# Values and output gates of a gated linear attention block as plain fp32 products by token rows, in place of three fp32r products of split weights

## Chip, cores and metric

One core of one Trainium2 chip. The metric is the device time of one execution in microseconds; the median of three runs of the kernel before is 1797.29 us (1794.79 to 1800.07).

## What is computed

A two-layer hybrid block, then a second two-layer block, on 256 tokens of width 1024, all in fp32. The change lies in one mixer of the second block, the gated linear attention (GLA), 4 heads with key width 128 and value width 256:

```python
def gla_mixer(h, w_in, w_alpha, b_alpha, norm_g, w_out):
    proj = h @ w_in
    q, k, v, r, z = jnp.split(proj, [GLA_QK, 2 * GLA_QK, 2 * GLA_QK + D_MODEL, 2 * GLA_QK + 2 * D_MODEL], axis=-1)
    log_alpha = jax.nn.log_sigmoid((z @ w_alpha + b_alpha).astype(jnp.float32)) / GLA_TAU
    ...
    o = gla_chunk_scan(q, k, v, log_alpha)
    o = rmsnorm_2(o, norm_g).reshape(bsz, s, D_MODEL).astype(h.dtype)
    return (o * jax.nn.silu(r)) @ w_out
```

`v` and `r` (the output gate) are each `h` (256 x 1024) times a 1024 x 1024 part of `w_in`.

## The kernel before

Activations lie in SBUF feature-major: `[128 partitions, feature tile k of 8, tokens]`. Dense products run as **three fp32r products**: an operand is split into a high half (fp32r, written by a cast) and a low half (the rest), and high x high, high x low and low x high are summed in PSUM.

**Weights.** SyncE streams 1 MB slabs of 256 output columns (`stream`, DMA at line 1273) into a ring of `RING = 3` slots, in the order of use; slab n waits until slab n - 3 is marked used (line 1272). A slab is two units of 128 columns. `split_to` on ScalarE copies a unit to `w_hi` (line 1314), `split_to` on VectorE writes `w_lo` (line 2025) and marks the slab used at its second half. There are `PARTS = 4` slots for halves: unit u waits until TensorE has used unit u - 4. `split_until(tile)` runs the split up to `AHEAD = 3` units ahead of a tile; an explicit `split_to(unit_of[...])` fixes the place in an engine's queue by hand. Every engine's queue is one list in program order; all waits are on counters of finished steps.

**TensorE's side.** `project(name, n)` (line 639, products at 653, 655, 658) waits for the unit's halves and makes a 128 x 256 result, feature-major, in 24 products. `open_bank` (line 586) takes the eight PSUM banks in turn and waits until the name eight before has been emptied. `keep_clock(n)` (line 598, products at 604) issues n plain fp32 products whose result nobody reads. `turn_tokens` (line 686, transposes at 691) transposes a 128-column tile into token rows.

**The GLA block, in TensorE's order.** `project_group` of glaq 0 to 2 with z (lines 1107 to 1123); the four `alpha` products (1128); glaq 3 and glak 0 to 3; then glav 0 to 7, each `project`, evacuated to `act_t`, turned by `turn_tokens` and evacuated to `gv`; then eight level products `lev` (lines 1139 to 1158, 1152 the main one) with a cross product per head (1162) and after every second one a gate chunk glar 0 to 3; then the head products `go` (1182, 1183), feature-major, with the sums of squares through a product by ones (`head_squares`, 1170); then glar 4 to 7; `keep_clock(7)`; and `block_out("gla")`, which is `rows_out` with `by_tile=True`: `two_chunks` (1008 to 1010) runs output chunks 0 and 1 tile by tile as the input tiles get ready, then the loop at 1039 to 1041 chunks 2 and 3. Then the boundary to the feed-forward, `gain_rows` and `ffn(1)`.

**ScalarE's side** (lines 1888 to 1943): z, then weight halves up to glak 1, Abs of the four alphas, Exp, Ln, and only then the evacuation of glaq 0 to 3 and of the keys; for the values an evacuation, the evacuation of the turned tile and one level factor's Exp (1913) each; Silu of the gates; copy and square of the heads (1930, 1931); the roots; Silu of gates 4 to 7; the high halves of the eight output tiles (1769).

**VectorE's side** (lines 2868 to 2959): log forget gates and their scans (2883, 2886), level differences (2902, 2903) and level factors (2911, 2912) with weight halves at fixed places between, masks and sums of the level products (2924 to 2934), four reciprocals of 128 x 256 (2940), the norm with gain (2944), the product with the gate (2953), the low halves (2033), and the storing of output rows.

Of the kernel before, what the change touches and what calls it, by code (L numbers as in the profile page):

```python
# [25 lines left out]
P = 128  # L26
# [86 lines left out]
def program(nc, io, counts):  # L113

    ctx = ExitStack()
    with ctx:
# [157 lines left out]
        yT, sq8 = carve(0, KT, S), carve(2048, KT, S)  # L274
# [10 lines left out]
        zT, scan_one = carve(17408, S), carve(17664, S)  # L285
        ff_act = carve(4096, FT, S)
# [242 lines left out]
        for n, c0, k in (("q", 0, 2), ("k", 512, 2), ("v", 1024, 4), ("r", 2048, 4)):  # L529
            for i in range(k):  # L530
                split_cols(f"w gla{n} {i}", [f"gla{n} {2 * i + j}" for j in range(2)], io["gla_w_in_2"][0],
                           c0 + 256 * i, "gla")
# [44 lines left out]
        def _(pe):  # L577
# [447 lines left out]
            def rows_out(tag, chunks, part, ready, by_tile):  # L1025
# [43 lines left out]
            def block_out(tag):  # L1069

                rows_out(tag, block_chunks(tag), lambda h, k: h[:, k, S:2 * S], both_parts(tag), True)
# [61 lines left out]
            for n in range(KT):  # L1133
                project(f"glav {n}", S)
                if n:
                    turn_tokens(f"glav {n - 1}", act_t[(n - 1) % 2], ST)
            turn_tokens(f"glav {KT - 1}", act_t[(KT - 1) % 2], ST)

            for n in range(GLA_H * ST):
# [24 lines left out]
                if n % 2 == 0:  # L1164
                    project(f"glar {n // 2}", S)
            def head_squares(hd):
                out = open_bank(f"gs {hd}")
                for e in range(2):
                    pe.wait_ge(*scalar.did(f"go {2 * hd + e}"))
                    m = pe.matmul(out[:, 0:S], ones_pp, sq8[:, 2 * hd + e, :], start=e == 0, stop=e == 1)  # L1170
                m.then_inc(*tensor.does(f"filled gs {hd}"))

            pe.wait_ge(*scalar.did("gv 7"))
            for hd in range(GLA_H):
# [3 lines left out]
                for e in range(2):  # L1178
                    name = f"go {2 * hd + e}"
                    out = open_bank(name)  # L1180
                    c = 256 * hd + P * e
                    pe.matmul(out[:, 0:S], gv[:, 0, c:c + P], attT[:, hd, 0, :], start=True, stop=False)
                    pe.matmul(out[:, P:S], gv[:, 1, c:c + P], attT[:, hd, 1, P:S], start=False, stop=True)\
                        .then_inc(*tensor.does("filled " + name))
                if hd:
                    head_squares(hd - 1)
            head_squares(GLA_H - 1)

            for n in range(KT // 2, KT):
                project(f"glar {n}", S)  # L1190
            keep_clock(7)
            block_out("gla")
# [99 lines left out]
        def _(act):  # L1292
# [614 lines left out]
            for i in range(8):  # L1907
                projected(f"glav {i}", act_t[i % 2][:, 0:S], also=[f"rows glav {i}"])
                if i:
                    evacuate(f"turned glav {i - 1}", gv[:, :, P * i - P:P * i], also=[f"gv {i - 1}"])  # L1910
                j = (7 + i) % 8
# [3 lines left out]
            evacuate(f"turned glav {KT - 1}", gv[:, :, D - P:D], also=[f"gv {KT - 1}"])  # L1915
            def r_out(n):
                projected(f"glar {n}", r_sil[:, n, :], ACT.Silu, [f"r_sil {n}"])
# [7 lines left out]
            warm_sqrt("gs")  # L1925
            for n in range(KT):
                name = f"go {n}"
                act.wait_ge(*tensor.did("filled " + name))

                nc.scalar.activation(gla_o[:, n, :], bank(name)[:, 0:S], ACT.Copy)  # L1930
                nc.scalar.activation(sq8[:, n, :], bank(name)[:, 0:S], ACT.Square)\
                    .then_inc(*scalar.does(name, "emptied " + name))
            for hd in range(GLA_H):
                evacuate(f"gs {hd}", act_t[hd][:, 0:S], ACT.Sqrt, [f"dev gs {hd}"], scale=1.0 / (2 * P), bias=eps)
            for n in range(KT // 2, KT):
                r_out(n)
            split_to(unit_of["y gla.3"])
            for n in range(KT):
                high_tile("gla", gla_o, "gla_y", n)
# [7 lines left out]
        def _(dve):  # L1947
# [931 lines left out]
            split_to(unit_of["glak 1"])  # L2879
# [4 lines left out]
            for hd in range(GLA_H):  # L2884
                after(f"lb {hd}")
                step(nc.vector.tensor_tensor_scan(gg[:, hd, :], scan_one, la[:, hd, :], 0.0, ALU.mult, ALU.add), f"gg {hd}")
            after(f"gg {GLA_H - 1}")
# [8 lines left out]
            for n, i in enumerate(level_order):  # L2896
                split_to(unit_of["glaq 0"] + 5 + n)
# [8 lines left out]
            for n, i in enumerate(level_order):  # L2906
                split_to(min(unit_of["glaq 0"] + 11 + n, unit_of["glar 1"]))
# [8 lines left out]
            for n in range(GLA_H * ST):  # L2916
                hd, t = n // ST, n % ST
                if n % 2 == 0:
                    split_for(f"glar {n // 2}")
# [16 lines left out]
            split_for(f"glar {KT // 2 - 1}")  # L2936
            settled()
            for hd in range(GLA_H):
                dve.wait_ge(*scalar.did(f"dev gs {hd}"))
                step(nc.vector.reciprocal(dve_t[hd][:, 0:S], act_t[hd][:, 0:S]), f"rinv gs {hd}")  # L2940
            split_for(f"glar {KT // 2}")
            for n in range(KT):
                after(f"rinv gs {n // 2}")
                step(nc.vector.scalar_tensor_tensor(gla_o[:, n, :], gla_o[:, n, :], param("gla_g")[:, n % 2:n % 2 + 1],
                                                    dve_t[n // 2][:, 0:S], ALU.mult, ALU.mult), f"gon {n}")
                if n == 3:
                    split_for(f"glar {KT // 2 + 1}")
            for n in range(KT):
                if KT // 2 + 1 < n:
                    split_for(f"glar {n}")  # L2950
                dve.wait_ge(*scalar.did(f"r_sil {n}"))
                after(f"gon {n}")
# [105 lines left out]
```

## Time and profile before

| | us |
|---|---|
| median of three runs (lowest, highest) | 1797.29 (1794.79, 1800.07) |
| the profiled execution, its own time | 1796.44 |
| span of that execution, first to last instruction | 1794.7 |
| TensorE busy (share of the span) | 1731.7 (96%) |
| VectorE busy | 1428.3 (80%) |
| ScalarE busy | 884.1 (49%) |
| weight streams, share of 16 engines' span | 50.7% |

The profile is of one execution. A matmul record's duration holds its latency; what a product costs in a run of them is the distance of the starts. A plain fp32 product shows as two records, an fp32r product as one. The clock column is the granted clock of TensorE as a share of 2.4 GHz.

### The profile page before, as it was taken

Reading aid. Unit: us, or ns where it says so; the run is one execution under the profiler, and the core shown is the slowest. Engines: PE = TensorE matmul, PEld = TensorE weight load, DVE = VectorE, ACT = ScalarE, POOL = GpSimd, SP = SyncE. Lnnn points to the kernel's source line nnn. Section 1 sums busy time; section 2 is a strip of 40 time slices with the busy share of each in tenths; the row PEclk is TensorE's granted clock in tenths of the full one; section 3 lists DMA queues with packets and bytes.
Section 4 is the critical chain, followed back from the end, with each engine's and each line's share of the span. In section 5 each row is a group of like instructions: output and inputs, shape, how many; then the busy total and the mean of one; then the engine's idle time right before and its main releaser. Section 6 shows DMA issues by size and latency. Waiting matters only on the chain.

```text
span 1794.7 us, 29926 instructions
## 1 busy us (share of the span) xinstructions
PE 1731.7 (96%) x11446; PEld 1536.0 (86%) x11446; DVE 1428.3 (80%) x2579; ACT 884.1 (49%) x1560; POOL 0.2 (0%) x4
## 2 busy tenths in 40 slices
PE   6999999999999999999999999998999989999998
PEld 3788887767888887888978999988999989899998
DVE  7799996558899898887876899877988468768874
ACT  4322334456223233453356745676666466556653
POOL 0000000000000000000000000000000000000000
PEclk9999999999999999999999999999999999999999
DMA  9583321211767776643522499544555535236553
GB/s 341 194 289 109 94 71 32 87 37 63 265 231 252 256 253 214 206 149 117 165 71 84 143 339 311 193 147 142 164 190 174 179 118 165 94 103 204 188 171 112
DMA packets 242189, 301.44 MB, mean 168 GB/s; under 512 B 6000, under 2 KB 223472, under 8 KB 241664
## 3 DMA queue, kind: packets, MB, share of 16 engines
q1 hardware_dynamic: 242048, 299.52, 50.7%
q8 instruction: 93, 1.52, 0.4%
q14 instruction: 48, 0.39, 0.1%
HBM read 298.45 MB, written 1.05 MB: 167 GB/s over the span
## 4 chain that ended last, share of the span: by engine, by line
PE 44%; DVE 7%; ACT 3%; issue 2%; DMA 0%; DVEq 0%; ACTq 0%
PE bank L653 10%; PE bank L655 10%; PE bank L658 10%; PE bank L1039 2%; PE bank L1040 2%; PE bank L1041 2%; DVE w_lo L2025 2%; ACT w_hi L1314 1%; PE bank L629 1%; PE bank L630 1%; PE bank L631 1%; DVE xT L2659 0%; PE bank L874 0%; PE bank L1093 0%; PE bank L897 0%
## 5 line engine op out<-in xcount | busy, mean ns | idle before, releaser
L2025 DVE TENSOR_TENSOR w_lo<-ring,w_hi 128x1024 fp32r<-128x1024 f32 (+2 forms) x444 | 499.4, 1133 | 184.5 <-ACT w_hi L1314 183.4
L1314 ACT ACTIVATE w_hi<-ring 128x1024 fp32r<-128x1024 f32 (+2 forms) x444 | 432.5, 984 | 179.6 <-PE bank L658 97.7
L653 PE MATMUL bank<-h_hi,w_hi 128*128 128x256 f32 (+2 forms) x2270 | 406.3, 321 | 3.9 <-ACT arena L1300 3.6
L655 PE MATMUL bank<-h_lo,w_hi 128*128 128x256 f32 (+2 forms) x2270 | 397.7, 317 | 0.0
L658 PE MATMUL bank<-h_hi,w_lo 128*128 128x256 f32 (+2 forms) x2270 | 396.8, 316 | 0.1
L653 PEld LDWEIGHTS bank<-h_hi,w_hi 128*128 128x128 f32 x2270 | 333.7, 189 | 39.6 <-ACT arena L1300 4.8
L655 PEld LDWEIGHTS bank<-h_lo,w_hi 128*128 128x128 f32 x2270 | 334.5, 189 | 29.8
L658 PEld LDWEIGHTS bank<-h_hi,w_lo 128*128 128x128 f32 x2270 | 333.3, 188 | 30.2 <-DVE w_lo L2025 0.5
L1300 ACT ACTIVATE work<-bank 128x512 f32<-128x512 f32 (+1 forms) x142 | 70.3, 512 | 257.5 <-PE bank L658 204.6
L1300 ACT ACTIVATE arena<-bank 128x256 f32<-128x256 f32 (+4 forms) x125 | 56.4, 454 | 206.9 <-PE bank L658 147.5
L2332 DVE SCALAR_TENSOR_TENSOR arena<-arena,params 128x512 f32<-128x512 f32 (+1 forms) x240 | 130.3, 610 | 0.0
L2062 DVE CUSTOM_DVE_ANT_0 arena<-arena,c_row,params 128x1024 f32<-128x1024 f32 x96 | 119.8, 1279 | 3.2 <-DMA arena<-in_ada_w_t 3.2
L1039 PE MATMUL bank<-w_hi,h_hi 128*128 128x256 f32 x320 | 90.0, 281 | 2.9 <-ACT w_hi L1314 2.6
L1300 ACT ACTIVATE work<-bank,params 128x256 f32<-128x256 f32 x88 | 49.5, 563 | 85.6 <-DVE w_lo L2025 43.1
L1041 PE MATMUL bank<-w_hi,h_lo 128*128 128x256 f32 x320 | 90.0, 281 | 0.0
L1040 PE MATMUL bank<-w_lo,h_hi 128*128 128x256 f32 x320 | 89.9, 281 | 0.0
L653 PE MATMUL bank<-arena_r,w_hi 128*128 128x512 f32 (+2 forms) x306 | 64.8, 338 | 1.9 <-ACT w_hi L1314 1.7
L2735 DVE SCALAR_TENSOR_TENSOR work<-bank,params,work 128x255 f32<-128x255 f32 x88 | 42.3, 481 | 29.2 <-ACT work L1300 29.2
L655 PE MATMUL bank<-arena_r,w_hi 128*128 128x512 f32 (+2 forms) x306 | 64.6, 337 | 0.0
L658 PE MATMUL bank<-arena_r,w_lo 128*128 128x512 f32 (+2 forms) x306 | 64.5, 337 | 0.0
L1039 PEld LDWEIGHTS bank<-w_hi,h_hi 128*128 128x128 f32 x320 | 60.2, 188 | 3.7 <-ACT w_hi L1314 3.0
L2058 DVE CUSTOM_DVE_ANT_0 arena<-arena,tables,params 128x1024 f32<-128x1024 f32 x48 | 60.5, 1279 | 0.0
(312 smaller groups left out, 2292.0 us busy)
## 6 DMA issues: line engine op xcount, KB each, us to landing
ring<-in_w_in SPq DMA_DIRECT2D x86, 1024.0 KB, 5.8
arena<-in_ada_w_t SPq DMA_DIRECT2D x96, 512.0 KB, 6.0
ring<-in_ffn_w_up SPq DMA_DIRECT2D x44, 1024.0 KB, 5.1
ring<-in_w_branch SPq DMA_DIRECT2D x32, 512.0 KB, 4.9
arena<-in_w_mod_t SPq DMA_DIRECT2D x32, 512.0 KB, 5.5
ring<-in_ffn_w_down SPq DMA_DIRECT2D x16, 1024.0 KB, 5.1
ring<-in_gla_w_in SPq DMA_DIRECT2D x12, 1024.0 KB, 5.3
ring<-in_w_out SPq DMA_DIRECT2D x8, 1024.0 KB, 6.4
```

The source lines that it names most:

```text
L653: pe.matmul(out[:, 0:n], w[0][:, k, :], hi(k, n), start=k == 0, stop=False)
L655: pe.matmul(out[:, 0:n], w[0][:, k, :], lo(k, n), start=False, stop=False)
L658: m = pe.matmul(out[:, 0:n], w[1][:, k, :], hi(k, n), start=False, stop=k == tiles - 1)
L1039: pe.matmul(out, part(h_hi, k)[:, rows], hi, start=k == 0, stop=False)
L1040: pe.matmul(out, part(h_hi, k)[:, rows], lo, start=False, stop=False)
L1041: return pe.matmul(out, part(h_lo, k)[:, rows], hi, start=False, stop=k == k1 - 1 and k1 == chunks(c)[-1][1])
L1300: return nc.scalar.activation(dst, src, func, **kw)\
L1314: nc.scalar.activation(w_hi[u % PARTS][:, 0:src.shape[1], :], src, ACT.Copy)\
L2025: step(nc.vector.tensor_tensor(w_lo[u % PARTS][:, 0:nk, :], src, w_hi[u % PARTS][:, 0:nk, :].bitcast(F32), ALU.subtract), f"lo {u}", *(["u ...
L2058: step(nc.vector.tensor_tensor_reduce(w if v else scratch, w, c_rows[:, v, :], 1.0, param("b_mod", 2)[:, l, c:c + 1], ALU.mult, ALU.add, m ...
L2062: step(nc.vector.tensor_tensor_reduce(w, w, c2_row, 1.0, param("ada_b", 2)[:, l, c:c + 1], ALU.mult, ALU.add, mod2[l][:, c:c + 1]), name)
L2332: step(nc.vector.scalar_tensor_tensor(dst, src, cw[:, l, k, n:n + 1], dst, ALU.mult, ALU.add), name)
```

## The change

- The slabs of values and gates are no longer split: they are put in the stream as they are, without units, and TensorE marks them used.
- `project_rows(kind, i)`: token rows t of chunk c (256 columns) as 8 plain fp32 products, the normed activations `pair_tile(k)` stationary and the slab moving; the result is already by token rows, 128 x 256. All values (8) and all gates (8) go so; the transposes of the values go.
- Heads are computed by token rows, 3 products of 256 columns each. Their sums of squares come from ScalarE's accumulator over a row, so root and reciprocal are on 128 x 8. The gate and the norm are one VectorE step from PSUM (for head 3 two steps).
- The heads are turned back by transposes (`head_turned`), between gates 5, 6, 7, and for head 3 inside the first output chunk; high and low halves are made from PSUM with the norm gain. `keep_clock(7)` goes. `block_out` uses the plain chunk loop for all four chunks (`by_tile` false).
- ScalarE empties glaq 0 to 2 ahead of the alphas; the weight halves of the keys stand at other places; ScalarE's and VectorE's splits for values and gates go.

```diff
-        gla_o = carve(4096, KT, S)
+        gla_o = carve(4096, ST, D)
-        r_sil = carve(11264, KT, S)
+        r_sil = carve(11264, ST, D)
...
+                if n in "vr":
+                    stream.append((f"w gla{n} {i}", by_rows(io["gla_w_in_2"][0])[:, :, c0 + 256 * i:c0 + 256 * i + 256], (8, 256)))
+                else:
+                    split_cols(f"w gla{n} {i}", [f"gla{n} {2 * i + j}" for j in range(2)], io["gla_w_in_2"][0],
+                               c0 + 256 * i, "gla")
...
+                        early = k1 - 2 if between and c == 0 else k0
+                        for t in range(ST if early > k0 else 0):
+                            for k in range(k0, early):
+                                if t == 0:
+                                    ready(k)
+                                products(k, t)
+                            if t == 0:
+                                between()
                         for t in range(ST):
-                            for k in range(k0, k1):
+                            for k in range(early, k1):
...
-            for n in range(KT):
-                project(f"glav {n}", S)
-                if n:
-                    turn_tokens(f"glav {n - 1}", act_t[(n - 1) % 2], ST)
-            turn_tokens(f"glav {KT - 1}", act_t[(KT - 1) % 2], ST)
+            def project_rows(kind, i):
+                c, t = i // ST, i % ST
+                w = take(f"w {kind} {c}")
+                out = open_bank(f"{kind} {i}")
+                for k in range(KT):
+                    m = pe.matmul(out[:, 0:2 * P], pair_tile(k)[:, P * t:P * t + P], w[:, k, :],
+                                  start=k == 0, stop=k == KT - 1)
+                m.then_inc(*tensor.does(f"filled {kind} {i}", *([f"used w {kind} {c}"] if t == ST - 1 else [])))
+            for i in range(GLA_H * ST):
+                project_rows("glav", i)
...
-                    project(f"glar {n // 2}", S)
+                    project_rows("glar", n // 2)
+            def head_turned(hd):
+                pe.wait_ge(*vector.did(f"gla_y {hd}.{ST - 1}"))
+                for n in range(2 * hd, 2 * hd + 2):
+                    out = open_bank(f"gla turned {n}")
+                    for t in range(ST):
+                        m = pe.transpose(out[:, P * t:P * t + P], gla_o[:, t, P * n:P * n + P], ident)
+                    m.then_inc(*tensor.does(f"filled gla turned {n}"))
...
+                pe.matmul(out[:, 0:256], attT[:, hd, 0, 0:P], gv[:, 0, v], start=True, stop=True)
+                pe.matmul(out[:, 256:512], attT[:, hd, 0, P:S], gv[:, 0, v], start=True, stop=False)
+                pe.matmul(out[:, 256:512], attT[:, hd, 1, P:S], gv[:, 1, v], start=False, stop=True)\
+                    .then_inc(*tensor.does(f"filled go {hd}"))
+            project_rows("glar", 4)
+            project_rows("glar", 5)
+            head_turned(0)
+            head_turned(1)
+            project_rows("glar", 6)
+            head_turned(2)
+            project_rows("glar", 7)
+            block_out("gla", lambda: head_turned(GLA_H - 1))
```

ScalarE:

```diff
-            split_to(unit_of["glak 1"])
+            split_to(unit_of["glak 0"])
+            for n in range(GROUP):
+                q_out(n)
             for hd in range(GLA_H):
                 evacuate(f"alpha {hd}", le[:, hd, :], ACT.Abs, [f"le {hd}"], last=False,
                          bias=param("gla_b")[:, hd:hd + 1])
+            split_to(unit_of["glak 1"])
...
+            split_to(unit_of["glak 2"])
...
+            split_to(unit_of["glak 3"])
+            q_out(GROUP)
             for n in range(GLA_H):
-                projected(f"glaq {n}", gq[:, n, :], also=[f"gq {n}"], scale=GLA_DK ** -0.5)
-            for n in range(GLA_H):
-                projected(f"glak {n}", gk[:, n, :], also=[f"gk {n}"])
+                evacuate(f"glak {n}", gk[:, n, :], also=[f"gk {n}"])
+            level_exp(0)
+            level_exp(1)
+            for i in range(8):
+                evacuate(f"glav {i}", gv[:, i % 2, rows_of(i)], also=[f"gv {i}"])
+                if i < 3:
+                    level_exp(2 * i + 2)
+                    level_exp(2 * i + 3)
...
+                    nc.scalar.activation(act_t[t][:, 0:S], bank(f"go {hd}")[:, 256 * t:256 * t + 256], ACT.Square,
+                                         accum_out=head_sums[:, i:i + 1]).then_inc(*scalar.does(f"head sum {i}"))
+            act.wait_ge(*scalar.did("head sum 7"))
+            nc.scalar.activation(head_dev, head_sums, ACT.Sqrt, scale=1.0 / (2 * P), bias=eps).then_inc(*scalar.does("head dev"))
+            r_out(4)
+            r_out(5)
+            for n in range(4):
+                turned_high(n)
             split_to(unit_of["y gla.3"])
+            r_out(6)
+            turned_high(4)
+            turned_high(5)
+            r_out(7)
+            turned_high(6)
+            turned_high(7)
```

VectorE (the `split_to` and `split_for` calls between differences, factors, level products, norm and gate are taken out):

```diff
+            dve.wait_ge(*scalar.did("head dev"))
+            step(nc.vector.reciprocal(head_inv, head_dev), "head inv")
...
+            for hd in range(2):
+                for t in range(ST):
+                    head_scaled(hd, t)
+            for t in range(ST):
+                last_head(t)
+            for t in range(ST):
+                head_scaled(2, t)
+            for n in range(4):
+                turned_low(n)
             split_to(unit_of["y gla.3"])
+            last_gated(0)
+            turned_low(4)
+            turned_low(5)
+            last_gated(1)
+            turned_low(6)
+            turned_low(7)
```

`head_scaled` takes a head's bank times the reciprocal times the Silu of the gate into `gla_o`; `turned_high` and `turned_low` make the halves of a turned bank times the norm gain; `last_head` and `last_gated` do head 3 in two steps.

## Rows read from the trace of the kernel before

**Rows 1.** The page: the span, and busy time of each engine.

```profile
span 1794.7 us, 29926 instructions
...
PE 1731.7 (96%) x11446; PEld 1536.0 (86%) x11446; DVE 1428.3 (80%) x2579; ACT 884.1 (49%) x1560; POOL 0.2 (0%) x4
```

**Rows 2.** Busy time of each engine by stretch of the GLA block.

```profile
core 0: us, PE busy (x) PEld busy (x) DVE busy (x) ACT busy (x) POOL busy (x), PEclk, DMA share, GB/s
...
1468.50:1488.10 19.60, 16.04 (x121) 15.86 (x121) 16.70 (x26) 13.16 (x24) 0.00 (x0) 0.91 0.35 108
1488.10:1515.60 27.50, 24.83 (x212) 24.39 (x210) 23.18 (x32) 23.38 (x37) 0.00 (x0) 1.00 0.62 192
1515.60:1539.30 23.70, 23.70 (x344) 22.21 (x345) 19.34 (x41) 8.34 (x18) 0.00 (x0) 0.93 0.27 90
1539.30:1548.00 8.70, 8.70 (x50) 7.71 (x49) 1.97 (x6) 7.25 (x22) 0.00 (x0) 1.00 0.01 2
1548.00:1559.50 11.50, 11.50 (x99) 11.47 (x98) 11.50 (x14) 7.11 (x11) 0.00 (x0) 1.00 0.25 80
1559.50:1566.30 6.80, 3.18 (x17) 2.50 (x15) 6.80 (x14) 5.12 (x11) 0.00 (x0) 1.00 0.39 127
1566.30:1591.00 24.70, 24.55 (x193) 24.37 (x194) 12.58 (x24) 9.33 (x23) 0.00 (x0) 0.93 0.46 151
```

**Rows 3.** Who TensorE waited for from 1440 to 1640 us: total, times, longest.

```profile
PE bank L1008 <- DVE h_lo L2033: 3.6, 1, 3.6
PE bank L653 <- ACT arena L1300: 3.6, 1, 3.6
PE bank L1152 <- ACT w_hi L1314: 2.4, 1, 2.4
```

**Rows 4.** Engine busy time in three shorter stretches, columns as rows 2.

```profile
1475.17:1478.66 3.49, 3.49 (x17) 3.49 (x18) 3.46 (x7) 2.56 (x5) 0.00 (x0) 0.51 0.06 16
1567.40:1570.70 3.30, 3.30 (x18) 3.30 (x17) 1.13 (x4) 0.00 (x0) 0.00 (x0) 0.50 0.90 305
1171.70:1191.00 19.30, 15.12 (x71) 12.45 (x70) 13.21 (x25) 14.66 (x31) 0.00 (x0) 1.00 0.12 37
```

**Rows 5.** TensorE in order of time: start, duration, line, tiles, records.

```profile
1479.61 1.11 PE L653 MATMUL bank<-h_hi,w_hi 128*128 128x256 f32 x8
...
1488.13 1.11 PE L653 MATMUL bank<-h_hi,w_hi 128*128 128x256 f32 x8
...
1493.81 0.38 PE L691 MATMUL bank<-tables,work 128*128 128x128 f32 x2
1493.95 1.19 PE L653 MATMUL bank<-h_hi,w_hi 128*128 128x256 f32 x8
...
1521.16 0.92 PE L1152 MATMUL bank<-arena 128*64 128x64 f32 x24
...
1523.73 1.21 PE L653 MATMUL bank<-h_hi,w_hi 128*128 128x256 f32 x8
...
1526.75 0.92 PE L1152 MATMUL bank<-arena 128*64 128x64 f32 x24
...
1559.48 3.19 PE L604 MATMUL bank<-tables 128*128 128x256 f32 x14
```

**Rows 6.** Groups of instructions, 1455 to 1600 us: busy us, mean ns.

```profile
L2025 DVE TENSOR_TENSOR w_lo<-ring,w_hi 128x1024 fp32r<-128x1024 f32 x33 | 39.9, 1218 | 16.9 <-ACT w_hi L1314 16.8
L1314 ACT ACTIVATE w_hi<-ring 128x1024 fp32r<-128x1024 f32 x32 | 33.3, 1053 | 13.5 <-PE bank L1010 10.1 <-PE bank L1041 3.4
...
L2902 DVE TENSOR_TENSOR arena<-arena 128x512 f32<-128x512 f32 x8 | 5.5, 685 | 0.0
...
L2940 DVE RECIPROCAL work<-work 128x256 f32<-128x256 f32 x4 | 6.6, 1710 | 6.7 <-ACT work L1300 6.7
```

**Rows 7.** Weight slabs (line 1273), 1400 to 1600 us, from issue.

```profile
DMA to landing us min/median/max: 4.3/5.2/6.8
```

**Rows 8.** ScalarE in order of time.

```profile
1471.76 1.28 ACT L1900 ACT_TABLE_LOAD   x1
```

More of the change, by code:

```diff
@@ L1023, in two_chunks, with rows_out @@
                         products(1, k, t)
-            def rows_out(tag, chunks, part, ready, by_tile):
+            def rows_out(tag, chunks, part, ready, by_tile, between=None):
                 if by_tile:
@@ L1177, in _ @@
                 pe.wait_ge(*scalar.did(f"cross {hd}"))
[L1178 to L1192, printed above, removed]
+                out = open_bank(f"go {hd}")
+                v = slice(256 * hd, 256 * hd + 256)
+                pe.matmul(out[:, 0:256], attT[:, hd, 0, 0:P], gv[:, 0, v], start=True, stop=True)
[10 more added lines that the diff above has]
+            block_out("gla", lambda: head_turned(GLA_H - 1))
             gain_rows("ffn 1")
@@ L1924, in _ @@
                     r_out(n // 2)
[L1925 to L1932, printed above, removed]
-            for hd in range(GLA_H):
-                evacuate(f"gs {hd}", act_t[hd][:, 0:S], ACT.Sqrt, [f"dev gs {hd}"], scale=1.0 / (2 * P), bias=eps)
-            for n in range(KT // 2, KT):
-                r_out(n)
-            split_to(unit_of["y gla.3"])
-            for n in range(KT):
-                high_tile("gla", gla_o, "gla_y", n)
+            for hd in range(GLA_H):
+                for t in range(ST):
+                    i = ST * hd + t
+                    act.wait_ge(*tensor.did(f"filled go {hd}"))
+                    if i:
+                        act.wait_ge(*scalar.did(f"head sum {i - 1}"))
+                    nc.scalar.activation(act_t[t][:, 0:S], bank(f"go {hd}")[:, 256 * t:256 * t + 256], ACT.Square,
[6 more added lines that the diff above has]
+                turned_high(n)
+            split_to(unit_of["y gla.3"])
+            r_out(6)
[4 more added lines that the diff above has]
+            turned_high(7)
             warm_sqrt("gla")
@@ L2948, in _ @@
[L2948 to L2952, printed above, removed]
-                step(nc.vector.tensor_tensor(gla_o[:, n, :], gla_o[:, n, :], r_sil[:, n, :], ALU.mult), f"gla_y {n}")
-            split_to(unit_of["y gla.3"])
-            for n in range(KT):
-                low_part(f"gla.{n}", h_lo[:, n, S:2 * S], gla_o[:, n, :], h_hi[:, n, S:2 * S])
+            dve.wait_ge(*scalar.did("head dev"))
@@ new lines, in _, with head_scaled @@
+            step(nc.vector.reciprocal(head_inv, head_dev), "head inv")
+            after("head inv")
+            def head_scaled(hd, t):
+                i = ST * hd + t
+                v = slice(256 * hd, 256 * hd + 256)
+                dve.wait_ge(*scalar.did(f"r_sil {i}"))
+                step(nc.vector.scalar_tensor_tensor(gla_o[:, t, v], bank(f"go {hd}")[:, 256 * t:256 * t + 256],
+                                                    head_inv[:, i:i + 1], r_sil[:, t, v], ALU.mult, ALU.mult),
+                     f"gla_y {hd}.{t}", *([f"emptied go {hd}"] if t == ST - 1 else []))
@@ new lines, in turned_low, with last_head @@
+            def turned_low(n):
+                dve.wait_ge(*scalar.did(f"hi gla.{n}"))
+                step(nc.vector.scalar_tensor_tensor(h_lo[:, n, S:2 * S], bank(f"gla turned {n}")[:, 0:S],
+                                                    param("gla_g")[:, n % 2:n % 2 + 1], h_hi[:, n, S:2 * S].bitcast(F32),
+                                                    ALU.mult, ALU.subtract), f"lo gla.{n}", f"emptied gla turned {n}")
+            def last_head(t):
+                i, v = ST * 3 + t, slice(768, 1024)
+                step(nc.vector.tensor_scalar(gla_o[:, t, v], bank("go 3")[:, 256 * t:256 * t + 256], head_inv[:, i:i + 1],
+                                             None, ALU.mult), f"last head {t}", *(["emptied go 3"] if t == ST - 1 else []))
@@ new lines, in last_gated @@
+            def last_gated(t):
+                v = slice(768, 1024)
+                dve.wait_ge(*scalar.did(f"r_sil {ST * 3 + t}"))
+                after(f"last head {t}")
+                step(nc.vector.tensor_tensor(gla_o[:, t, v], gla_o[:, t, v], r_sil[:, t, v], ALU.mult), f"gla_y 3.{t}")
+            for hd in range(2):
[3 more added lines that the diff above has]
+                last_head(t)
+            for t in range(ST):
+                head_scaled(2, t)
```

53 lines of the change are left out of this document (18 added, 35 removed).

## The prediction

> **What bounds the kernel now.** I read the page first: TensorE is busy 96% of the span [rows 1], so a microsecond is worth something only if it leaves TensorE's queue or an idle gap in it. Then the stretches of the gated linear attention (GLA) block [rows 2]. Read there the gap between a stretch's length and its PE column, and the granted clock: three stretches lose idle time (3.6, 2.7 and 3.6 us), and three show a clock of 0.91 to 0.93. Then who ended the idle gaps [rows 3]: 3.6 us for a bank that ScalarE empties late, 2.4 us ahead of the level products, 3.6 us for the low halves ahead of the output projection. Each gap is followed by a stretch of work at a granted clock of 0.51 and 0.50, 1.2 GHz instead of 2.4 [rows 4] (two of the three are shown; the third falls into the levels). Last the order of time on TensorE [rows 5], for the price of each kind of product. ScalarE and VectorE are not the bound as sums, but they hand over late at these three places.
>
> **Two prices.** A `project` (24 fp32r products, 256 columns, a 128x256 result) repeats every (1488.13 - 1479.61)/3 = 2.84 us, or 0.118 us a product [rows 5]. A plain fp32 product of 256 columns is two records; fourteen records of `keep_clock` take 3.19 us, so one record is (3.19 - 0.38)/13 = 0.216 us and a product 0.432 us [rows 5]. `project_rows` does 8 of them for a result of the same size: 3.46 us. So each of the 16 value and gate chunks becomes 0.62 us **dearer** on TensorE, 9.9 us in all. The recurrent block runs such products with the ring as an operand at clock 1.00 [rows 4], so I take full speed.
> The Trainium skill (FP8 and Floating Point Precision, TensorE Precision Notes) says that true fp32 takes four passes through the array, where the change gives up three. That speaks against the change; the two records of 0.216 us agree in kind, at 0.432 us against 3 x 0.118 = 0.354 us.
>
> **Part by part**, on the path through TensorE.
> 1. Queries and keys, 19.6 us from 1468.5 to 1488.1 [rows 2]. ScalarE now empties glaq 0 to 2 ahead of Abs, Exp and Ln, so glak 0 finds its bank free, and the 3.6 us gap and the slow stretch behind it go. Does the next weight half come late instead? By ScalarE's order: glak 1's high half ends near 1470.1, then a table load of 1.28 us [rows 8], Exp, glak 2's half near 1473.8, load, Ln, glak 3's half near 1477.6. TensorE, running through, wants them at 1474.2, 1477.1 and 1479.9. VectorE's low half of glak 3 waits for the scans, near 1480.6; the third pass wants it at 1481.8. All hold, the last by 1.2 us. Five tiles x 2.84 = 14.2: **-5.4 us**.
> 2. Values, 27.5 us from 1488.1 to 1515.6 [rows 2]: 8 x 3.46 = 27.7 us, without eight pairs of transposes (0.14 us each [rows 5]) and the 2.7 us of gaps. **+0.2 us**. The level factors must be ready at 1510.4: VectorE starts the differences near 1480.6, and 32 half-tile steps at a pitch near 0.6 us (0.685 us long each [rows 6]) end near 1500. Ten microseconds to spare, since its weight halves of 1.22 us [rows 6] have left.
> 3. Levels with gates 0 to 3, 23.7 us [rows 2]: gates +4 x 0.62 = 2.5 us; the slow start goes. The first level and gate take 5.6 us there (1515.6 to 1521.2), against 3.0 for a gate (1523.7 to 1526.8) and 1.1 for a level at full clock [rows 5]: -1.5 us. **+1.0 us**.
> 4. Head products, 8.7 us [rows 2]: four heads x three products x 0.432 = 5.2 us. The eight products of the sums of squares (3.5 us) go to ScalarE. **-3.5 us**.
> 5. Gates 4 to 7, 11.5 us [rows 2]: 13.8 us, 12 transposes x 0.07 = 0.8 us between them, and one wait: gate 6 takes go 2's bank, which VectorE frees only after gate 5's Silu, some 0.7 us late. **+3.9 us**.
> 6. Clock keeping and the wait for the low halves, 6.8 us [rows 2, 3]: both go. The chain behind the heads loses four reciprocals of 1.71 us [rows 6] for one on eight columns, and is now cut into heads: 0 to 2 are ready under gates 6 and 7. **-6.8 us**.
> 7. Output projection, 24.7 us [rows 2]: 192 products x 0.118 = 22.65 us, the last head's four transposes 0.3 us, some 0.4 us for tiles 4 and 5 and the last head, 0.4 us as now at chunk changes; about 1.5 us of it was the slow stretch at 1567 to 1571 [rows 4]. **-0.9 us**.
> The 16 halves taken from ScalarE (1.05 us) and VectorE (1.22 us) [rows 6] count nothing themselves: TensorE's products hide them; they are the slack on which 1, 2 and 6 live. **Slabs**: the value and gate slabs are now held until TensorE has used them, 6.9 us each. A ring of three leaves two slabs' work, about 13.8 us, for a transfer of 4.3 to 6.8 us [rows 7], so no starvation. SyncE's queue has one critical place: output slab 1 is issued when gate 5 is done (1547.3) and lands near 1552.5. Behind it ScalarE waits with halves 2 and 3, and queued behind those is gate 6's Silu, then tiles 4 and 5: ready near 1557.5, when TensorE, which starts at 1555.8, has four tiles of the chunk done.
> Sum: -5.4 + 0.2 + 1.0 - 3.5 + 3.9 - 6.8 - 0.9 = **-11.5 us**. The feed-forward behind it shifts as it stands. The profiled execution took 1796.4 us around a span of 1794.7, 0.9 us under the median of 1797.3. So 1784.9 for that execution, 1785.8 as a median.
> Bounds of what no row shows: the gap in part 5 is between 0 and 1.5 us; the handovers in 7 between 0 and 5 us; the plain pitch with the ring's 1 KB rows as the moving operand between 0.432 and 0.472 us (next part).
>
> **Rivals.**
> A. **The last heads hand over late** (0.12). Against: the estimate above with a median landing. For: four engines pass the last two heads around, and each wait of today's block ended on just such a handover [rows 3]. A landing of 6.8 us instead of 5.2 [rows 7] costs 1.6 us at tiles 4 and 5; the same again for a second exposed hop of head 3, and if the gaps bring half clock, 1.5 us as today, make 4.7 with a table load of 1.28 [rows 8] 6.0 us: 1791.8.
> B. **Plain products cost four times the fp32r pitch** (0.05): 4 x 0.118 = 0.472 us, 16 x 8 x 0.040 = 5.1 us more: 1790.9. Against: the measured 0.216 a record [rows 5]. The rule of four passes in the Trainium skill (FP8 and Floating Point Precision) would give this if each pass had the fp32r overhead; the row shows that it has not.
> C. **Slower: the granted clock falls in the plain stretches** (0.05). Place: values and gates, 16 x 3.46 = 55 us of plain products. Each microsecond of full-clock work costs one more at 1.2 GHz, so it eats the gain from 11.5 us of it, and over 0.3% is reached at 17. If the eight values run so: +27.7, 1813. For: every gap in this block was followed by half clock [rows 4]. Against: products of this kind ran at 1.00 through gaps of 2 us [rows 4], and the new stretch has none.
> D. **The front gains nothing** (0.08): a half of glak 1 to 3 is late by what the bank was. The 1.2 us margin of part 1 is the thin one; if the Ln chain is 3 us later, 1.8 us and the half clock of 1.6 us come back, and part of the 2.4 us gap ahead of the levels: some 5 us, 1790.8.
> That the change does not do what it says I leave out: the order of each queue is written out.
>
> **Numbers.** Forecast 0.70, A 0.12, D 0.08, B 0.05, C 0.05. A measurement of this kernel can tell about 0.3%, 5.4 us, from no change: faster means under 1791.9. The forecast case, with handovers of up to 5 us and spread of the runs (1794.8 to 1800.1) around it, lies there with 0.67 of its 0.70; D and B with 0.09 of 0.13; A with half of 0.12: 0.82. Same 0.13, slower 0.05. Range: 1781.5 (no gap anywhere, 2 us of spread, and the slow stretches and changes of chunk all gone) to 1792.5 (A and the better part of D and B).
>
> **What would show it.** Right: records of the new products 0.216 us apart at clock 1.00; no wait of TensorE over 1 us between 1455 and the output projection's end, which falls near 1579.5 instead of 1591; level products from 1510, heads from 1535, the output projection from 1556; weight halves 16 fewer on both engines. Wrong: a wait on w_hi or w_lo in the keys (D), on gla_o, h_lo or w_hi around tiles 4 to 7 (A), a pitch near 0.236 (B), a clock under 0.9 in the values (C).

## The result and the profile after

The changed kernel takes **1785.39 us** in the median (1782.98 to 1786.30, four runs) against 1797.32 (1794.79 to 1800.07) for the kernel before: a ratio of 0.9931, 95% interval 0.9913 to 0.9949. That is 11.9 us less, where 11.5 were forecast. The profiled execution has a span of 1784.3 us against 1794.7. Its GLA block begins 1.5 us later than in the execution before. That start also varies between kernels that differ in nothing ahead of the block: the first alpha product stands at 1466.13 to 1469.09 in three variants of the changed kernel (exponentials spread, last head turned early, clock keeping put back, all below). So the block is best read by its own length: from the first product of glaq 3 to the first of the gain rows it is 122.5 us before (1468.51 to 1590.97) and 110.6 after (1469.98 to 1580.61), -11.8 us. What follows the block takes 203.7 us in both. The two block lengths come from one profiled execution each.

The page of the changed kernel, the lines that answer to [rows 1], and the two groups of weight halves:

```profile
span 1784.3 us, 29504 instructions
...
PE 1732.5 (97%) x11280; PEld 1530.7 (86%) x11280; DVE 1402.2 (79%) x2554; ACT 865.0 (48%) x1532; POOL 0.2 (0%) x4
...
L2075 DVE TENSOR_TENSOR w_lo<-ring,w_hi 128x1024 fp32r<-128x1024 f32 (+2 forms) x428 | 479.7, 1129 | 183.2 <-ACT w_hi L1336 181.9
L1336 ACT ACTIVATE w_hi<-ring 128x1024 fp32r<-128x1024 f32 (+2 forms) x428 | 415.5, 981 | 177.1 <-PE bank L662 98.7
```

TensorE is busy for 1732.5 us, not for less than before; its share rose because the span fell. The two engines that make the halves have 16 fewer each (444 before).

Busy time by stretch, as [rows 2] (columns as there):

```profile
core 0: us, PE busy (x) PEld busy (x) DVE busy (x) ACT busy (x) POOL busy (x), PEclk, DMA share, GB/s
1469.98:1484.20 14.22, 14.22 (x122) 14.22 (x121) 10.76 (x18) 10.23 (x19) 0.00 (x0) 1.00 0.30 86
1484.20:1511.92 27.72, 27.72 (x131) 24.13 (x129) 17.11 (x29) 11.91 (x17) 0.00 (x0) 1.00 0.46 147
1511.92:1536.70 24.78, 24.78 (x313) 21.10 (x313) 13.99 (x36) 6.34 (x17) 0.00 (x0) 1.00 0.29 87
1536.70:1541.88 5.18, 5.18 (x26) 4.57 (x25) 1.75 (x5) 3.16 (x13) 0.00 (x0) 1.00 0.58 200
1541.88:1557.27 15.39, 15.18 (x77) 13.24 (x76) 9.63 (x17) 10.93 (x20) 0.00 (x0) 1.00 0.21 68
1557.27:1581.00 23.73, 23.73 (x202) 23.70 (x201) 13.22 (x24) 11.97 (x27) 0.00 (x0) 1.00 0.75 236
```

Each length stands beside its PE column and a clock of 1.00: no gap and no slow stretch is left, but for 0.2 us. The stretches answer to keys, values, levels, heads, gates 4 to 7 and output projection (the last row runs 0.4 us on into the gain rows, which begin at 1580.61); the stretch of clock keeping and waiting, 6.8 us in [rows 2], no longer exists.

Who TensorE waited for, 1440 to 1640 us, as [rows 3]:

```profile
PE bank L994 <- DVE stats L2715: 1.8, 3, 0.8
PE bank L633 <- ACT h_hi L1777: 1.4, 2, 1.0
PE bank L633 <- ACT xT L1322: 0.5, 2, 0.3
PE bank L1151 <- DVE arena L2993: 0.2, 1, 0.2
```

The three gaps of [rows 3] are gone; what is left in the block is the 0.2 us for go 2's bank. The other three lines are the norm boundaries, in both kernels alike.

TensorE in order of time (a plain product is two records):

```profile
1484.20 27.79 PE L1151 MATMUL bank<-ring,work 128*128 128x256 f32 x128
1511.92 0.92 PE L1171 MATMUL bank<-arena 128*64 128x64 f32 x24
...
1548.79 1.04 PE L1192 MATMUL bank<-tables,arena 128*128 128x128 f32 x8
1550.04 3.69 PE L1151 MATMUL bank<-ring,work 128*128 128x256 f32 x16 [0.21 <-DVE arena L2993]
```

The values are 128 records, 64 products, in 1511.92 - 1484.20 = 27.72 us: 0.433 us a product, 0.2166 a record. The levels follow at once.

### The profile page after: what moved, and what is told of

It is laid out like the page before. It is cut to its first block, busy times and chain, and to the rows that moved or that the text cites. A ratio compares the mean times of both kernels' runs of the same rounds, so it can differ in the third digit from the quotient of the medians.

```text
span 1784.3 us, 29504 instructions
## 1 busy us (share of the span) xinstructions
PE 1732.5 (97%) x11280; PEld 1530.7 (86%) x11280; DVE 1402.2 (79%) x2554; ACT 865.0 (48%) x1532; POOL 0.2 (0%) x4
## 4 chain that ended last, share of the span: by engine, by line
PE 46%; DVE 6%; ACT 3%; issue 2%; DMA 0%; DVEq 0%; ACTq 0%
PE bank L657 9%; PE bank L662 9%; PE bank L659 9%; PE bank L1151 3%; PE bank L1043 3%; PE bank L1044 3%; PE bank L1045 3%; DVE w_lo L2075 2%; ACT w_hi L1336 1%; PE bank L633 1%; PE bank L634 1%; PE bank L635 1%; PE bank L1105 1%; DVE xT L2709 0%; PE bank L878 0%
## 5 line engine op out<-in xcount | busy, mean ns | idle before, releaser
L2075 DVE TENSOR_TENSOR w_lo<-ring,w_hi 128x1024 fp32r<-128x1024 f32 (+2 forms) x428 | 479.7, 1129 | 183.2 <-ACT w_hi L1336 181.9
L1336 ACT ACTIVATE w_hi<-ring 128x1024 fp32r<-128x1024 f32 (+2 forms) x428 | 415.5, 981 | 177.1 <-PE bank L662 98.7
L657 PE MATMUL bank<-h_hi,w_hi 128*128 128x256 f32 (+2 forms) x2142 | 385.8, 322 | 0.3
L662 PE MATMUL bank<-h_hi,w_lo 128*128 128x256 f32 (+2 forms) x2142 | 379.0, 319 | 0.0
L659 PE MATMUL bank<-h_lo,w_hi 128*128 128x256 f32 (+2 forms) x2142 | 378.9, 318 | 0.0
L657 PEld LDWEIGHTS bank<-h_hi,w_hi 128*128 128x128 f32 x2142 | 315.9, 188 | 35.5 <-issue 2.7
L659 PEld LDWEIGHTS bank<-h_lo,w_hi 128*128 128x128 f32 x2142 | 317.0, 188 | 29.8
L662 PEld LDWEIGHTS bank<-h_hi,w_lo 128*128 128x128 f32 x2142 | 317.0, 188 | 29.7
L1045 PEld LDWEIGHTS bank<-w_hi,h_lo 128*128 128x128 f32 x352 | 66.3, 188 | 0.0
L1044 PEld LDWEIGHTS bank<-w_lo,h_hi 128*128 128x128 f32 x352 | 66.2, 188 | 0.0
```

The lines of the kernel that those rows point to most:

```text
L657: pe.matmul(out[:, 0:n], w[0][:, k, :], hi(k, n), start=k == 0, stop=False)
L659: pe.matmul(out[:, 0:n], w[0][:, k, :], lo(k, n), start=False, stop=False)
L662: m = pe.matmul(out[:, 0:n], w[1][:, k, :], hi(k, n), start=False, stop=k == tiles - 1)
L1044: pe.matmul(out, part(h_hi, k)[:, rows], lo, start=False, stop=False)
L1045: return pe.matmul(out, part(h_lo, k)[:, rows], hi, start=False, stop=k == k1 - 1 and k1 == chunks(c)[-1][1])
L1336: nc.scalar.activation(w_hi[u % PARTS][:, 0:src.shape[1], :], src, ACT.Copy)\
```

## The experiments

Each run is read by its block, from the first alpha product to the gain rows: 124.38 us in the kernel before, 112.55 in the changed one. Each block length is that of one profiled execution. The median of the runs stands beside it where there were several, with its ratio to the kernel before and the 95% interval; the changed kernel's is 0.9931, 0.9913 to 0.9949. Where an interval overlaps this one, the medians don't tell the two kernels apart, and the reading rests on the traces.

### Query banks emptied late again

```diff
-            split_to(unit_of["glak 0"])
-            for n in range(GROUP):
-                q_out(n)
+            split_to(unit_of["glak 1"])
             for hd in range(GLA_H):
                 evacuate(f"alpha {hd}", ...)
...
-            split_to(unit_of["glak 3"])
+            for n in range(GROUP):
+                q_out(n)
+            split_to(unit_of["glak 2"])
             q_out(GROUP)
+            split_to(unit_of["glak 3"])
```

> The changed kernel with one part undone: ScalarE empties the first three query banks behind Abs, Exp and Ln again, and the key halves stand where they stood. Theory (the gap and the half clock behind it were worth 5.4 us, apart from the plain products): the stretch from glaq 3 to the end of glak 3 grows from 14.2 to 19.6 us, with one wait of about 3.6 us for ScalarE and a clock near 0.5 for some 3 us behind it; levels, heads and output stretch stay as they are; the block +5.4, the median near 1790.8. Rival (the 10 us that VectorE had to spare ahead of the level products absorb it): same stretch, but nothing at the end, median 1785. Second rival: the later order of the key halves makes it worse than before, over +7 us.

Block 117.90 us, **+5.35** (in the profiled execution it begins some 5 us late, at 1473.5, which is why the block and not the span is read); median 1789.52 (ratio to before 0.9964, 0.9949 to 0.9979). The third products of glaq 3 and glak 0 after it, on TensorE:

```profile
1482.11 1.50 PE L657 MATMUL bank<-h_hi,w_hi 128*128 128x256 f32 x8 [3.56 <-ACT arena L1322]
1483.40 1.91 PE L659 MATMUL bank<-h_lo,w_hi 128*128 128x256 f32 x8
1485.11 1.59 PE L662 MATMUL bank<-h_hi,w_lo 128*128 128x256 f32 x8
1486.54 1.10 PE L657 MATMUL bank<-h_hi,w_hi 128*128 128x256 f32 x8
```

The gap is 3.56 us, and the tile behind it takes 1486.54 - 1482.11 = 4.43 us where it takes 2.82 at full clock. 3.56 + 1.61 accounts for 5.2 of 5.35. Nothing later absorbs it, although VectorE idles for 14.55 us until the first level product is there (11.86 in the changed kernel): TensorE is the chain, and VectorE's slack is no slack of TensorE's. The medians agree in direction, 1789.52 against 1785.39; their intervals touch. The step of the prediction stands at its full price.

### The kernel before, with only the query banks emptied early

```diff
-            split_to(unit_of["glak 1"])
+            split_to(unit_of["glak 0"])
+            for n in range(GROUP):
+                evacuate(f"glaq {n}", gq[:, n, :], also=[f"gq {n}"], scale=GLA_DK ** -0.5)
+            split_to(unit_of["glak 1"])
...
-            for n in range(GLA_H):
+            for n in range(GROUP, GLA_H):
                 projected(f"glaq {n}", ...)
```

> The kernel before with one part of the change alone: the first three query banks are emptied ahead of the alphas; values and gates stay three fp32r products. Theory (VectorE, busy with weight halves and level steps, is what the level products then wait for): the gap at glak 0 goes, TensorE reaches the end of the values 5.4 us earlier, but waits there 3 to 5 us for the level factors instead of 2.4; the block ends 3 to 5 us earlier, median 1792.3 to 1794.3. Rival (the front gain is independent of the plain products): the whole 5.4 us arrive, median 1791.9. Second rival: nothing arrives, VectorE is the bound already.

Block 120.60 us, -3.78 against the kernel before; median 1792.35 (0.9975, 0.9966 to 0.9984). Within the range of the first theory, but not in the place that it named. TensorE's waits in the block, then VectorE just ahead of the levels:

```profile
PE bank L1008 <- DVE h_lo L2036: 3.6, 1, 3.6
PE bank L1152 <- ACT w_hi L1314: 2.4, 1, 2.4
PE bank L658 <- DVE w_lo L2028: 1.4, 1, 1.4
```

```profile
1508.10 0.67 DVE L2915 TENSOR_TENSOR arena<-arena 128x512 f32<-128x512 f32 x1
1509.13 0.69 DVE L2914 TENSOR_TENSOR arena<-arena 128x512 f32<-128x512 f32 x1 [0.36 <-ACT arena L1916]
1509.74 0.69 DVE L2915 TENSOR_TENSOR arena<-arena 128x512 f32<-128x512 f32 x1
1510.34 2.35 DVE L2028 TENSOR_TENSOR w_lo<-ring,w_hi 128x1024 fp32r<-128x1024 f32 x2
```

The gap ahead of the levels is the same 2.4 us, at an earlier time; the new loss is 1.4 us on a key's low half. From 1472.94 on, VectorE stands idle once, for the 0.36 us ahead of 1509.13, where before it stood idle for 4.3 us in that stretch. So VectorE is full: of 5.2 us in front, 3.8 arrive. Making the key's low half sooner would not help in this order, since VectorE's steps up to the last factor would end at the same time (read from the trace, not run). Alone, the reordering brings a third of the change; the rest of its own worth needs VectorE relieved.

### The exponentials spread again

```diff
-            level_exp(0)
-            level_exp(1)
             for i in range(8):
                 evacuate(f"glav {i}", gv[:, i % 2, rows_of(i)], also=[f"gv {i}"])
-                if i < 3:
-                    level_exp(2 * i + 2)
-                    level_exp(2 * i + 3)
+                level_exp(i)
```

> The changed kernel with ScalarE's eight level exponentials spread again, one behind the evacuation of each value chunk, as in the kernel before. Theory (in the kernel before the 2.4 us gap ahead of the level products hung on ScalarE's order as well as on VectorE's load: the last exponential stands behind the last value): evacuation 0.3, exponential 1.0, last two level steps 1.2, so TensorE waits 2.4 to 2.9 us ahead of the levels although VectorE carries no weight halves; with a slower clock behind it of 0.3 to 1.6 us, the block +2.7 to +4.5 us against the changed kernel. Rival (the gap came from VectorE's weight halves alone): no wait, +0.

Block 115.64 us, **+3.09**; median 1786.93 (0.9953, 0.9936 to 0.9969). TensorE and VectorE around the end of the values:

```profile
1507.74 2.32 PE L1151 MATMUL bank<-ring,work 128*128 128x256 f32 x10
1513.12 0.92 PE L1171 MATMUL bank<-arena 128*64 128x64 f32 x24 [3.05 <-DVE arena L2957]
```

```profile
1508.01 0.69 DVE L2956 TENSOR_TENSOR arena<-arena 128x512 f32<-128x512 f32 x1 [2.16 <-ACT arena L1943]
1508.62 0.68 DVE L2957 TENSOR_TENSOR arena<-arena 128x512 f32<-128x512 f32 x1
1511.46 0.69 DVE L2956 TENSOR_TENSOR arena<-arena 128x512 f32<-128x512 f32 x1 [2.16 <-ACT arena L1943]
1512.07 0.68 DVE L2957 TENSOR_TENSOR arena<-arena 128x512 f32<-128x512 f32 x1
```

From the fourth factor on VectorE waits 2.16 us ahead of each for ScalarE's exponential (2.03 ahead of the third). It carries no weight halves in this stretch, and TensorE waits 3.05 us. The kernel before shows the same wait, 1.75 us, ahead of its last factor:

```profile
1513.94 0.69 DVE L2911 TENSOR_TENSOR arena<-arena 128x512 f32<-128x512 f32 x1 [1.75 <-ACT arena L1913]
1515.59 1.07 PE L1152 MATMUL bank<-arena 128*64 128x64 f32 x24 [2.41 <-ACT w_hi L1314]
```

The second line, like [rows 3], names a weight half on ScalarE as what ended the gap. But the level products wait in the code for the factors and not for that half. TensorE starts 0.36 us after the last factor's end here (1515.23) and 0.37 us after it in the run above (1512.75), so it is the factor.

So plain products alone would not have closed the gap of [rows 3] ahead of the levels: the exponentials had to leave their places behind the value evacuations as well. The prediction credited VectorE's relief alone ("since its weight halves have left"). In the changed kernel the factors are complete at 1501.3, and VectorE next moves when the first level product is there:

```profile
1500.64 0.67 DVE L2961 TENSOR_TENSOR arena<-arena 128x512 f32<-128x512 f32 x1
1513.17 0.62 DVE L2971 TENSOR_TENSOR arena<-bank,tables 128x448 f32<-128x448 f32 x1 [11.86 <-PE bank L1175]
```

### Clock keeping: taken from the kernel before, put back into the changed one

```diff
-            keep_clock(7)
             block_out("gla")
```

> The kernel before without the seven clock-keeping products ahead of the output projection. Theory (the wait for the low halves ends at the same time whoever fills it, so that the 6.8 us between gate 7 and the projection are one chain on ScalarE and VectorE): the wait grows from 3.6 to 6.6 us, the projection starts at the same time, and costs up to 3 us more at half clock; block +0 to +3 us. Rival (the clock-keeping products cost their 3.0 us): the block 2 to 3 us shorter.

Block 124.90 us, +0.52; median 1796.96 (1.0011, 1.0001 to 1.0020). The last products of gate 7 and the first of the output projection:

```profile
1557.89 1.10 PE L658 MATMUL bank<-h_hi,w_lo 128*128 128x256 f32 x8
1565.63 0.55 PE L1008 MATMUL bank<-w_hi,h_hi 128*128 128x256 f32 x1 [6.64 <-DVE h_lo L2032]
1565.98 0.41 PE L1009 MATMUL bank<-w_lo,h_hi 128*128 128x256 f32 x1
```

The wait grows from 3.6 to 6.64 us and the projection begins 99.60 us after the alphas, 99.69 before: one chain through ScalarE and VectorE set that time, and the seven products only filled it. They saved 0.5 us, in clock: without them the first 4.4 us of the projection ran at a granted clock of 0.50, where [rows 4] has 3.3 us at that clock.

```diff
+            keep_clock(7)
             block_out("gla", lambda: head_turned(GLA_H - 1))
```

> The changed kernel with the seven clock-keeping products put back ahead of the output projection. Theory (nothing waits there any more): all of 14 x 0.216 = 3.0 us is added, less at most the 0.2 us of waits at the first chunk; the block +2.8 to +3.0 us. Rival (they cover a wait as they did in the kernel before, spread over small gaps that the profile does not show): +0 to +1.5 us.

Block 115.58 us, **+3.03**; one execution, 1790.03.

```profile
1558.49 3.19 PE L608 MATMUL bank<-tables 128*128 128x256 f32 x14
```

The products' whole 3.0 us are paid, because nothing is left for them to cover. Together the two runs show that the 6.8 us of part 6 went because the chain got shorter, not because the products were dropped. Which of its links did it (the four reciprocals, the weight halves gone from VectorE's queue, the cut by head) was not separated, but for the last head, next.

### The last head turned ahead of the output projection

```diff
-            block_out("gla", lambda: head_turned(GLA_H - 1))
+            head_turned(GLA_H - 1)
+            block_out("gla", lambda: None)
```

> The changed kernel with head 3 turned ahead of the output projection instead of inside its first chunk. Theory (gla_y of head 3 is ready 1.6 us after TensorE has finished gate 7): one wait of 1.6 to 1.8 us on VectorE ahead of the transposes, and up to 1 us for tiles 6 and 7 behind them: the stretch from gate 7 to the end of the projection +1.6 to +2.7 us. Rival (tiles 4 and 5 would have been late anyway, so the order only moves the wait): +0 to 0.5 us. Rival (a gap there brings half clock): +3 or more.

Block 114.15 us, **+1.60**; one execution, 1787.96.

```profile
1559.27 0.66 PE L1192 MATMUL bank<-tables,arena 128*128 128x128 f32 x4 [1.33 <-DVE arena L3016]
```

1.33 us of idle time stand in the profile, counted from the end of gate 7's last record, which holds its latency. From start to start it is more: the transposes begin 4.95 us after gate 7 does (1554.32), where the projection of the changed kernel begins 3.27 us after it (1554.00 to 1557.27). That is 1.68 us, which covers the 1.60. No slow clock follows it (the next products start 0.12 us apart). The six tiles of chunk 0 that run first are a real cover, and a small one.

### Gates as three fp32r products by token rows

```diff
+                if f"{kind} {2 * c}" in unit_of:
+                    units = [unit(f"{kind} {2 * c + j}") for j in range(2)]
+                    slot = unit_of[f"{kind} {2 * c}"] % PARTS
...
+                        pe.matmul(o, a_hi, hi, start=k == 0, stop=False)
+                        pe.matmul(o, a_hi, lo, start=False, stop=False)
+                        m = pe.matmul(o, a_lo, hi, start=False, stop=k == KT - 1)
```

The halves of gate slab 0 are made while the values run, those of slabs 1 to 3 during the levels, those of output slab 1 behind gate 7.

> The changed kernel, but all eight gate chunks by token rows as three fp32r products of split weights (high and low halves of the activations stationary, two units of halves moving). Theory (a plain chunk costs TensorE 3.46 us, three fp32r passes 2.84, and both other engines have room in the levels and the tail): the levels and the stretch of gates 4 to 7 lose 8 x 0.62 = 5.0 us, the block -4 to -5 us against the changed kernel, median 1780.4 to 1781.4. Rival (handovers: halves of the gates and of the first output units now stand in the queues of the last heads): gaps of 2 to 5 us ahead of gates 6, 7 or the output projection, with half clock behind them, no gain: 1785 or more.

Block 107.63 us, **-4.92** against the changed kernel; median 1779.97 (0.9901, 0.9886 to 0.9916). Levels, heads and gates 4 to 7 of this kernel:

```profile
1511.96:1534.27 22.31, 22.31 (x346) 20.86 (x346) 18.75 (x40) 10.64 (x22) 0.00 (x0) 1.00 0.60 191
1534.27:1539.45 5.18, 5.18 (x27) 4.56 (x26) 4.12 (x7) 4.28 (x16) 0.00 (x0) 1.00 0.00 0
1539.45:1552.40 12.95, 12.74 (x108) 12.53 (x107) 8.57 (x18) 9.06 (x18) 0.00 (x0) 1.00 0.29 94
```

The levels take 22.31 us for 24.78 and the gates 12.95 for 15.39, still at clock 1.00. Per chunk 4.92 / 8 = 0.615 us, the forecast difference of 0.62, now by exchange. The median's interval overlaps the changed kernel's at its edge (0.9916 against 0.9913). For the gates the plain form was a pure cost: both other engines had the room for 8 more halves each.

### And the last two value slabs, or all four

The same form of product for value slabs 2 and 3, their halves made between the level steps.

> As gates_r, and the last two of the four value slabs also as three fp32r products (four chunks). Theory (VectorE has 10.7 us to spare ahead of the level products, four more halves take 4.9): another 4 x 0.62 = 2.5 us off the values, no wait ahead of the levels, median near 1778. Rival (the halves in the middle of the level steps come late for their chunk): waits on w_lo of 1 to 3 us in the values, gain gone.

Block 105.18 us, **-7.37**; median **1776.84** (1776.29 to 1779.61; 0.9888, 0.9873 to 0.9903), whose interval lies wholly below the changed kernel's. Against the kernel with the gates alone the block is 2.45 us shorter, and the medians don't settle it (the intervals overlap). The stretch of its values:

```profile
1485.14:1510.41 25.27, 25.27 (x162) 23.48 (x160) 23.94 (x35) 17.50 (x23) 0.00 (x0) 1.00 0.65 204
```

25.27 us for 27.72. VectorE is now busy for 23.9 of them, so little of what it had to spare is left. Its last factor is complete at 1506.8, 3.6 us ahead of the first level product at 1510.4; a pair of halves for the gates fills 2.4 us of that.

> As gates_r, and all four value slabs as three fp32r products, by token rows. Theory (the plain products pay where VectorE is short): VectorE then needs 8 x 1.2 + 19.3 = 29 us from the end of the scans, TensorE only 22.7 for the values, so TensorE waits 3 to 6 us ahead of the level products or on w_lo in the values, with half clock behind it (1.5): the stretch of the values 27 to 30 us including the wait, no better than the plain one (27.7) and worse than gates_values_r by 2 to 5 us. Rival (TensorE is the only bound): 22.7 us, the block -9.9 against the changed kernel, median 1775.5.

Block 115.29 us, +2.74 against the changed kernel and +10.1 against the last; median 1786.97 (0.9945, 0.9928 to 0.9962). The waits of TensorE in its values, and the whole stretch:

```profile
1481.92 0.36 PE L1156 MATMUL bank<-w_hi,h_hi 128*128 128x256 f32 x1 [4.01 <-DVE w_lo L2104]
...
1490.55 0.36 PE L1156 MATMUL bank<-w_hi,h_hi 128*128 128x256 f32 x1 [1.19 <-DVE w_lo L2104]
...
1500.04 0.55 PE L1156 MATMUL bank<-w_hi,h_hi 128*128 128x256 f32 x1 [3.59 <-DVE w_lo L2104]
```

```profile
1477.75:1513.10 35.35, 26.55 (x195) 25.93 (x193) 30.81 (x42) 21.28 (x27) 0.00 (x0) 0.90 0.48 147
```

Three waits on low halves, 8.8 us, and a mean clock of 0.90: 22.7 + 8.8 us of the 35.35. The other 3.9 us are mostly slow clock (0.63 over the 4.1 us behind the first wait, 0.66 over the 5.0 us behind the third). TensorE is not the only bound there. But the stretch was forecast at 27 to 30 us, and the excess is no measure of VectorE's work: two of the three waits come from where I put the halves in ScalarE's queue, behind the last key and behind the first value. VectorE stood idle for them:

```profile
1479.31 2.36 DVE L2104 TENSOR_TENSOR w_lo<-ring,w_hi 128x1024 fp32r<-128x1024 f32 x2 [3.70 <-ACT w_hi L1349]
1487.93 2.36 DVE L2104 TENSOR_TENSOR w_lo<-ring,w_hi 128x1024 fp32r<-128x1024 f32 x2 [1.44 <-ACT w_hi L1349]
```

How good an all-fp32r order placed with more care would be was not tried. An estimate from this trace: VectorE's last factor ends at 1509.28; without its 3.70 and 1.44 us of idle time it would end at 1504.1, while TensorE without a wait would be through the values at 1477.75 + 22.7 = 1500.5. So the values with the wait behind them would still take about 26.8 us (1504.1 + 0.4 - 1477.75), and more if the clock falls, against 25.27 for the mixed form and 27.72 for the plain one.

## Why the prediction was right

| part | length forecast | measured | change forecast | measured |
|---|---|---|---|---|
| 1 keys | 14.2 | 14.22 | -5.4 | -5.4 |
| 2 values | 27.7 | 27.72 | +0.2 | +0.2 |
| 3 levels, gates 0 to 3 | 24.7 | 24.78 | +1.0 | +1.1 |
| 4 heads | 5.2 | 5.18 | -3.5 | -3.5 |
| 5 gates 4 to 7 | 15.4 | 15.39 | +3.9 | +3.9 |
| 6 clock keeping and wait | 0 | 0 | -6.8 | -6.8 |
| 7 output projection | 23.8 | 23.34 | -0.9 | -1.4 |

- **The price of a plain product** (0.432 us, measured 0.433) and of a chunk (0.62 us more than three passes, by exchange 0.615) were the terms that could have turned the sign. Rival B, 0.472 us, is out, and with it the reading of the four passes of the Trainium skill (FP8 and Floating Point Precision, TensorE Precision Notes) as four times the fp32r pitch of this kernel.
- **Part 1** held with its margins (1.2 us forecast for the last): glak 3's low half ended at 1482.05, its third pass began at 1483.26. Its worth was confirmed by undoing it, its dependence on a relieved VectorE by doing it alone.
- **Part 2** was right in its sum and incomplete in its reason: the gap ahead of the levels needed ScalarE's new order too (3.05 us when it is undone). The change contained that order, so the number was safe; the prediction did not say why.
- **Part 5** was right by luck, as a sum of two slips of half a microsecond: the bank wait was 0.2 us, not 0.7, and the transposes ran at some 0.11 us each, not 0.07 (eight from 1548.79 in 1.04 us, less one latency). The rows had the dearer price already: with a pair of transposes in it, a value tile of [rows 5] repeats after some 3.05 us instead of 2.84 (1493.95 to 1496.99), so a pair cost 0.2 us and not 0.14.
- **Part 6** was the largest term, and the two clock-keeping runs show it as a shortened chain; how the shortening divides among its links stays open.
- **Part 7** was 0.5 us too dear: tiles 4 and 5 and the last head cost next to nothing. The queue that I named as critical was so on ScalarE, without reaching TensorE:

```profile
1554.00 2.00 ACT L1336 ACTIVATE w_hi<-ring 128x1024 fp32r<-128x1024 f32 x2 [1.28 <-DMA ring<-in_gla_w_out]
1555.91 0.37 ACT L1322 ACTIVATE arena<-bank 128x256 f32<-128x256 f32 x1
```

It waits 1.28 us for output slab 1, then empties gate 6 at 1555.9. TensorE came to tile 4 only at 1558.88; the low halves of tiles 4 and 5 had ended at 1558.58. Rival A did not happen, with 0.3 us to spare there.

- **Rival C**: the plain stretches ran at clock 1.00 throughout. Rival D did not happen.

The change moved little because it spent what it won: gaps, slow clock and removed products gave some 22 us, the 16 plain chunks took 9.9 of them. The runs say where they were not worth their price: for the gates and for value slabs 2 and 3 the passes of split weights were cheaper, 7.4 us in all. For value slabs 0 and 1 the plain form is the better of the orders that were run; against a better placed all-fp32r order only the estimate above speaks for it.

## What to carry to other kernels

Where one engine is busy 96% of the time, sum by its queue: every stretch of this block came out within 0.1 us from two pitches and the gaps, but for the last (and one of them by two slips that cancel). A dearer form of product can pay only for the chunks during which the engines that prepare the cheap form are full; price the exchange chunk by chunk, not for a whole projection. A filler product costs nothing exactly as long as the wait that it fills is there, so look at it again when the wait is gone.

## What was not expected

A gap of 3.05 us between plain products and the level products (exponentials spread) was followed by full clock:

```profile
1513.12:1517.81 4.69, 4.69 (x46) 3.93 (x46) 1.96 (x5) 0.00 (x0) 0.00 (x0) 1.00 0.38 129
```

The same place in the kernel before:

```profile
1515.59:1521.16 5.57, 5.57 (x54) 5.32 (x55) 3.79 (x7) 1.12 (x1) 0.00 (x0) 0.69 0.43 147
```

Gaps of 2.4 us at the same place behind transposes and fp32r products in the kernel before, and of 3.56 us in the keys (query banks late), were followed by clocks of 0.69 and 0.61 over the next 5.6 and 4.4 us. The kernel before with the query banks emptied early repeats the first of these (2.41 us, then 0.70). In the prediction every gap of this size in the block was taken to bring half clock. So the length of the gap alone does not decide it. One execution shows the exception; what makes the difference was not tested.
